# Loading the first weight chunks and inputs of both output stages from the stages ahead of them

## The reference, cut to what matters

```python
# first block
b = multiscale_pool(u_b, pool_w[layer], pool_scale[layer]) * jax.nn.silu(z_b)
g = jax.nn.sigmoid(gates.reshape(B, S, N_BRANCHES, D_MODEL) + merge_bias[layer])
y = g[:, :, 0] * (a @ w_branch_a[layer]) + g[:, :, 1] * (b @ w_branch_b[layer])
x = x + y @ w_out[layer]
# second block
merged = gate_a * (y_a @ w_proj_a[l]) + gate_b * (y_b @ w_proj_b[l])
y = merged @ w_out[l]
x = x + gate * _rms(y, g_post[l])
```

## Time and profile before

| | before |
|---|---|
| median of three runs | 3318.81 us (3316.91 to 3326.31) |
| profiled execution, its own time | 3323.57 us |
| its span | 3321.8 us |
| mean granted TensorE clock | 0.967 of full speed |
| PE busy | 3110.3 us, 94% |
| DVE, ACT, POOL busy | 1732.5, 1552.3, 956.3 us |
| out1 begins, out2 begins (SP's first DMA) | 1491.21, 2943.02 us |

### The profile page before, as it was taken

The page is one execution under the profiler, slowest core; times in us unless marked ns, Lnnn a source line. Parts: engine busy times, 40 slices in busy tenths (PEclk is TensorE's granted clock), DMA queues, the critical chain, the costliest instruction groups (busy, mean ns, idle before and its releaser), DMA issues. The chain is left out here.

```text
span 3321.8 us, 43017 instructions
## 1 busy us (share of the span) xinstructions
PE 3110.3 (94%) x15772; PEld 2529.6 (76%) x15772; DVE 1732.5 (52%) x3657; ACT 1552.3 (47%) x2448; POOL 956.3 (29%) x701
## 2 busy tenths in 40 slices
PE   8995999889995999997999799979999999989998
PEld 7994888768884677765778678868888888868787
DVE  6775799989996665536531166642211231133423
ACT  4544688756983677762111143324444354431111
POOL 3541012200222566642222133312322222212222
PEclk9996999999997999998999899989999999999999
DMA  5656333253334621106552345464344543355422
GB/s 177 206 182 231 96 96 100 80 189 110 100 102 155 198 78 51 39 20 192 155 146 93 131 150 161 140 212 142 114 131 137 197 125 118 119 152 157 133 102 89
DMA packets 431706, 440.63 MB, mean 133 GB/s; under 512 B 31008, under 2 KB 324256, under 8 KB 431392
## 3 DMA queue, kind: packets, MB, share of 16 engines
q1 hardware_dynamic: 431520, 438.18, 42.7%
HBM read 279.51 MB, written 158.60 MB: 132 GB/s over the span
## 5 line engine op out<-in xcount | busy, mean ns | idle before, releaser
L1342 PE MATMUL p_pr<-p_hT,p_w_hi 128*128 128x512 f32 x896 | 354.8, 396 | 16.1 <-POOL p_w_lo L1095 10.0
L1343 PE MATMUL p_pr<-p_hT,p_w_hi 128*128 128x512 f32 x896 | 352.3, 393 | 0.0
L1344 PE MATMUL p_pr<-p_hT,p_w_lo 128*128 128x512 f32 x896 | 352.0, 393 | 0.0
L1628 POOL TENSOR_TENSOR a_prob<-a_prob,a_inv 128x1024 f32<-128x1024 f32 (+12 forms) x104 | 250.7, 2419 | 211.2 <-DVE a_inv L1673 211.0
L1135 ACT ACTIVATE p_relu<-p_isc,p_level 128x2048 int8<-128x2048 f32 (+5 forms) x192 | 276.4, 1441 | 22.5 <-DVE p_level L1232 17.7
L791 PE MATMUL t_pj_ps<-t_w_hi,t_hT_slot 128*128 128x356 f32 (+2 forms) x768 | 272.2, 354 | 11.5 <-DVE t_w_lo L639 5.9
L1095 POOL TENSOR_TENSOR p_w_lo<-p_w_raw,p_w_hi 128x256 fp32r<-128x256 f32 x144 | 107.5, 777 | 603.7 <-DVE p_level L1232 399.6
L793 PE MATMUL t_pj_ps<-t_w_hi,t_hT_slot 128*128 128x356 f32 (+2 forms) x768 | 265.2, 345 | 0.0
L792 PE MATMUL t_pj_ps<-t_w_lo,t_hT_slot 128*128 128x356 f32 (+2 forms) x768 | 264.8, 345 | 0.0
L1648 DVE CUSTOM_DVE_ANT_0 a_prob<-a_s_ps,a_mask 128x512 f32<-128x512 f32 (+3 forms) x320 | 189.4, 607 | 141.2 <-PE a_s_ps L1782 136.5
L2260 PE MATMUL o_b_ps<-o_in_hi,o_w_hi 128*128 128x512 f32 x512 | 209.0, 408 | 39.5 <-DVE o_in_lo L2147 27.4
(11 more groups left out here) (291 smaller groups left out, 7120.4 us busy)
## 6 DMA issues: line engine op xcount, KB each, us to landing
s_hT<-t_hT_slot SPq DMA_DIRECT2D x32, 1024.0 KB, 5.9
s_gT<-p_o_sb SPq DMA_DIRECT2D x128, 256.0 KB, 4.9
o_gates<-s_gT SPq DMA_DIRECT2D x64, 512.0 KB, 5.1
p_w_raw<-in_w_in SPq DMA_DIRECT2D x56, 512.0 KB, 4.3
t2n_w_raw<-in_w_in SPq DMA_DIRECT2D x56, 512.0 KB, 4.2
s_qT<-t_qT_slot SPq DMA_DIRECT2D x32, 512.0 KB, 2.7
p_hT<-s_hT SPq DMA_DIRECT2D x32, 512.0 KB, 9.3
s_zuT<-p_o_sb SPq DMA_DIRECT2D x64, 256.0 KB, 4.8
```

Of the source, the lines that this page charges most:

```text
L1342: nc.tensor.matmul(pr[n % NPR][:], wh, hi, start=(k == 0), stop=False)
L1343: nc.tensor.matmul(pr[n % NPR][:], wh, lo, start=False, stop=False)
L1344: last = nc.tensor.matmul(pr[n % NPR][:], wl, hi, start=False, stop=(k == KD - 1))
L1628: nc.gpsimd.tensor_tensor(p, p, f, ALU.mult).then_inc(normed, 1)
```

## The change

1. The raw weights `w_raw` (32 KB a partition) and raw inputs `in_raw` (24 KB) of the output stages now lie at the start of the free memory, and are set aside in att1 and in second too, so that they cover tiles that die there: `w_ada`, `kT` and `qT` in att1, `hT0` and the split weights in second (for which `hT0` is now put ahead of them).
2. att1's SP, ahead of its last two stores, waits for all scores and then loads weights chunks 0 to 3 and a inputs 0 to 3 of out1: 8 + 4 DMAs of 256 KB. second's SP does the same for out2 ahead of its last three stores of gates, behind a wait for the last unit that reads `hT0` and for the last weight split.
3. The output stages don't load these any more. In out1 SP's order becomes: four u's (with the pooling weights behind the first), z 0 and 1, gates 0 and 1, z 2 and 3 (which wait for the first two mixes), chunks 4 to 7, four a inputs, and then at once the next group's u's and z 0, 1. For later groups the u's are issued in the turn of the last unit of the group before, one turn earlier than before.
4. In out2 the first four units now run as in out1, a halves first, and ACT and DVE split in the order that this needs.

```diff
+OPEN = 4
+RING = KD + KD // 2
+def merge_raw(c, tag):
+    with ExitStack() as shared:
+        sb, _, _ = c.alloc(shared, tag)
+        return sb("w_raw", [P, KD, D], F32), sb("in_raw", [P, RING, BANK], F32)
+def load_merge_weights(c, sp, n, second, landed):
+    for half, w in enumerate((c.w_proj_a_2, c.w_proj_b_2) if second else (c.w_branch_a, c.w_branch_b)):
+        sp.dma_start(c.merge_raw[0][:, half * KD // 2:(half + 1) * KD // 2, n * P:(n + 1) * P],
+                     w[0, :, n * P:(n + 1) * P].rearrange("(k p) n -> p k n", p=P)).then_inc(landed, 16)
+def load_merge_ahead(c, sp, second):
+    w_landed, a_landed = c.ahead[second]
+    for n in range(OPEN):
+        load_merge_weights(c, sp, n, second, w_landed[n])
+        sp.dma_start(c.merge_raw[1][:, n], c.aT[n][:, 0:BANK]).then_inc(a_landed[n], 16)
...
+                if turn == N_TURNS - 2:
+                    sp.wait_ge(scored, PIECES[N_TURNS])
+                    for s in (0, 1):
+                        sp.wait_ge(stored[s], 16 * GROUPS * NKV // 2)
+                    load_merge_ahead(c, sp, False)
                 sp.wait_ge(gated, turn + 1)
...
             if not second:
-                load_u(0, 0)
-                load_u(0, 1)
-            load_weights(0)
-            for x in range(KD):
-                load_src(x)
-            if not second:
-                sp.dma_start(w_pool.rearrange("c (g d) -> c g d", g=KB - 1), c.pool_w[0, 0:KB - 1].rearrange("g c d -> c g d")
-                             ).then_inc(wp_loaded, 16)
-                sp.dma_start(w_pool_last[:], c.pool_w[0, KB - 1]).then_inc(wp_loaded, 16)
-                load_weights(1)
-                load_u(0, 2)
-                load_u(0, 3)
+                for g in range(KB):
+                    load_u(0, g)
...
                 load_z(0, 0)
                 load_z(0, 1)
-            else:
-                load_weights(1)
+            for x in range(KB, KD):
+                load_src(x)
             load_gates(0)
-            load_weights(2)
             load_gates(1)
-            for n in range(3, KD):
-                load_weights(n)
             if not second:
                 load_z(0, 2)
                 load_z(0, 3)
+            for n in range(OPEN, KD):
+                load_weights(n)
             for x in range(KD, RING):
                 load_src(x)
+            if not second:
+                load_pool(1)
...
-                if not second and u < LAST and u % KD == 0:
-                    for g in range(KB):
-                        load_u(u // KD + 1, g)
-                    load_z(u // KD + 1, 0)
-                    load_z(u // KD + 1, 1)
+                if not second and u < LAST - KD and u % KD == KD - 1:
+                    load_pool(u // KD + 2)
...
-                if x == KB and not second:
+                if x == KB:
                     for n in range(1, OPEN):
                         high_weights(n)
...
                 low_merge(0)
-                for x in ON_DVE:
-                    low_input(x)
-                for n in range(1, KD):
+                low_input(0)
+                low_input(2)
+                for n in range(1, OPEN):
+                    low_merge(n)
+                low_input(4)
+                low_input(6)
+                for n in range(OPEN, KD):
                     low_merge(n)
...
-                if tg == 0 and not second:
-                    open_units(0, range(OPEN), 0)
+                if tg == 0:
+                    open_units(0, range(OPEN), None if second else 0)
...
+                if n == N_UNITS - 1:
+                    sp.wait_ge(unit_done, N_UNITS - LEAD)
+                    sp.wait_ge(w_lo_done, 2 * CHUNKS)
+                    for s in (0, 1):
+                        sp.wait_ge(a_stored[s], 16 * GROUPS * NKV // 2)
+                    load_merge_ahead(c, sp, True)
```

More of the change, by code:

```diff
@@ L208, in handed_on @@
     sb, _, _ = c.alloc(stack, name)
+    hT = [sb("hT0", [P, 2, KD, BANK], F32R)]
     w_raw = sb("w_raw", [P, 2, KD, P], F32)
@@ L211, in handed_on @@
     w_lo = sb("w_lo", [P, 3, KD, P], F32R)
-    hT = [sb(f"hT{g}", [P, 2, KD, BANK], F32R) for g in range(2)]
+    hT.append(sb("hT1", [P, 2, KD, BANK], F32R))
     return w_raw, w_hi, w_lo, hT
+OPEN = 4
[13 more added lines that the diff above has]
+        sp.dma_start(c.merge_raw[1][:, n], c.aT[n][:, 0:BANK]).then_inc(a_landed[n], 16)
 def pipeline(eng, stages, weights=None, later=None, ending=None):
@@ L1875, in phase_output @@
     tag = "r2" if second else "r1"
+    w_raw, in_raw = c.merge_raw
+    w_lo = sb("w_lo", [P, KD, D], F32R)
+    in_lo = sb("in_lo", [P, RING, BANK], F32R)
     yT = sb("yT", [P, T, KD, P], F32)
     w_hi = sb("w_hi", [P, KD, D], F32R)
-    with ExitStack() as shared:
-        w_raw = c.alloc(shared, tag)[0]("w_raw", [P, KD, D], F32)
-    w_lo = sb("w_lo", [P, KD, D], F32R)
     src = sb("src", [P, 2, BANK], F32)
@@ L1896, in phase_output @@
     x_out = gates[:].rearrange("p s b n -> p s (b n)")
-    w_loaded, w_hi_done, w_lo_done = [sem(f"w_loaded{n}") for n in range(KD)], sem("w_hi_done"), sem("w_lo_done")
-    raw_loaded = [sem(f"raw_loaded{x}") for x in range(RING)]
+    w_landed, a_landed = c.ahead[second]
+    w_loaded, w_hi_done, w_lo_done = w_landed + [sem(f"w_loaded{n}") for n in range(OPEN, KD)], sem("w_hi_done"), sem("w_lo_done")
+    raw_loaded = a_landed + [sem(f"raw_loaded{x}") for x in range(KB, RING)]
     src_loaded, g_loaded = [sem("s_even"), sem("s_odd")], [sem("g_even"), sem("g_odd")]
@@ L1966, in load_weights @@
             def load_weights(n):
-                for half, w in enumerate((wa, wb)):
-                    sp.dma_start(part(w_raw, n)[:, half * KB:(half + 1) * KB],
-                                 w[0, :, n * P:(n + 1) * P].rearrange("(k p) n -> p k n", p=P)).then_inc(w_loaded[n], 16)
+                load_merge_weights(c, sp, n, second, w_loaded[n])
             def load_gates(u):
@@ L1998, in load_z, with load_pool @@
                 sp.dma_start(z_pool[g % 2], c.zuT[8 + g][:, r * BANK:(r + 1) * BANK]).then_inc(z_loaded[g % 2], 16)
-            if not second:
-                load_u(0, 0)
-                load_u(0, 1)
-            load_weights(0)
-            for x in range(KD):
-                load_src(x)
-            if not second:
-                sp.dma_start(w_pool.rearrange("c (g d) -> c g d", g=KB - 1), c.pool_w[0, 0:KB - 1].rearrange("g c d -> c g d")
-                             ).then_inc(wp_loaded, 16)
-                sp.dma_start(w_pool_last[:], c.pool_w[0, KB - 1]).then_inc(wp_loaded, 16)
-                load_weights(1)
-                load_u(0, 2)
-                load_u(0, 3)
+            def load_pool(r):
+                for g in range(KB):
+                    load_u(r, g)
+                load_z(r, 0)
+                load_z(r, 1)
+            if not second:
+                for g in range(KB):
+                    load_u(0, g)
+                    if g == 0:
+                        sp.dma_start(w_pool.rearrange("c (g d) -> c g d", g=KB - 1), c.pool_w[0, 0:KB - 1].rearrange("g c d -> c g d")
+                                     ).then_inc(wp_loaded, 16)
+                        sp.dma_start(w_pool_last[:], c.pool_w[0, KB - 1]).then_inc(wp_loaded, 16)
                 load_z(0, 0)
                 load_z(0, 1)
-            else:
-                load_weights(1)
+            for x in range(KB, KD):
+                load_src(x)
             load_gates(0)
-            load_weights(2)
             load_gates(1)
-            for n in range(3, KD):
-                load_weights(n)
             if not second:
@@ L2102, in _ @@
                 if x == KD:
-                    for n in range(1 if second else OPEN, KD):
+                    for n in range(OPEN, KD):
                         high_weights(n)
@@ L2294, in _ @@
             for tg in range(GROUPS):
-                if tg == 0 and not second:
-                    open_units(0, range(OPEN), 0)
-                    pool_map(0, 2)
-                    pool_map(0, 3)
+                if tg == 0:
+                    open_units(0, range(OPEN), None if second else 0)
+                    if not second:
+                        pool_map(0, 2)
+                        pool_map(0, 3)
                     close_units(0, range(OPEN), None)
@@ L2381, in phase_second @@
     SCORES_AT, KEYS_AT, WEIGH_AT = 6, 9, 10
+    c.merge_raw = merge_raw(c, "r2")
     handed_on(c, stack, "p2n")
@@ L2786, in build_program @@
     c.x = c.x.rearrange("o s d -> (o s) d")
+    c.ahead = [([nc.alloc_semaphore(f"w_landed{second}{n}") for n in range(OPEN)],
+                [nc.alloc_semaphore(f"a_landed{second}{n}") for n in range(OPEN)]) for second in range(2)]
     with ExitStack() as keep:
```

8 lines of the change are left out of this document (2 added, 6 removed).

## The result

| | before | changed |
|---|---|---|
| median of six runs each, taken together | 3321.03 us (3316.91 to 3328.23) | 3305.16 us (3303.17 to 3308.65) |
| profiled execution, its own time | 3323.57 us | 3305.27 us |
| its span | 3321.8 us | 3303.5 us |
| mean granted TensorE clock | 0.967 | 0.969 |
| PE busy | 3110.3 us | 3107.1 us |

The changed kernel is faster by 15.9 us, a ratio of 0.995 with a 95% interval of 0.9939 to 0.9961. (out1's opening is from here on DVE's first instruction in it, 0.07 us behind SP's first DMA; out2's is SP's first DMA.)

A forecast was written before the change was run, and what follows sets the result against it. Out1's opening was taken as limited by late loads, splits and pooling, its body by PE. Gains of 16.3 us in out1 and 6.2 in out2 made 22.5, off 3318.8: 3296.3 us, own range 3292 to 3304, overall 3288 to 3308.

The forecast's parts named there:

- the wait for u: In out1's first group, DVE's 6.67 us wait for the next group's first u was to go.
- A: Rival: out1's stall only moves; chunk 7 lands 6 us later, gain 10 instead of 16; 3302.3 us, chance 0.14.
- the first product: DVE's first gate product in out1, forecast near 33 us after the opening.
- B: Rival: only the earlier starts of out1 and out2 are gained, 11 us; 3308 us, chance 0.11.
- the fifth product: DVE's fifth gate product in out1, forecast near 53 us after the opening.
- C: Rival: early loads hold att1's last store of `aT`, so att1 ends 33 us late; 3329 us, chance 0.03.
- D: Rival: early loads wait until their stage's end and land where they did; 0 to -6 us, 3316 us, chance 0.04.
- the collision: DVE and POOL splitting inputs together after each stage start: 0 extra taken, at most 3.0 us on DVE's chain in out1.
- The restart: PE's slow restart at out1's opening, kept as it was; staying at 2.4 GHz would give 2.7 us.

The follow-up runs named there:

- a: The changed kernel run again with no edit: 3304.99 us, 0.995 of before.
- i: The changed kernel run a third time, unaltered: 3302.7 us, 0.9941 of before.
- h: The kernel before the change, run once more: 3316.3 us (one run).
- c: The changed kernel with the change undone in att1 and out1, so kept for out2 only: 3315.77 us, 0.998 of before.
- b: The changed kernel with the change undone in second and out2, so kept for out1 only: 3308.78 us, 0.9962 of before.
- e: The changed kernel with all four first-group a inputs split on DVE, none on POOL, in both output stages: 3300.23 us, 0.9938 of before.
- f: The changed kernel with POOL's splits of out1's second-group a inputs held until the stage's sixth mix is done: 3300.54 us, 0.9939 of before.

## Why the prediction was right, and where its sum was off

**The mechanism held.** The early loads are issued where they should be, ahead of the stores and at no cost to them; ACT starts with the stage; the wait for u is gone; out1 and out2 add up. A is not there: ACT waits 0.85 us for chunk 7, until 1522.48, and the first product is 30.9 us after the opening, ahead of the 32.7 forecast, mostly because the late chunks landed 4.8 us after their issue and not 6.1. B is out by the fifth product, 15.1 us earlier against the opening, C by the 3.40 us between att1's last product and out1's opening, D by the loads.

**By stages.** In the two profiles the gain is 18.3 us of the 22.5 that the sum took off the profiled execution: out1 14.8 for 16.3, out2 6.0 for 6.2, and the stages ahead of out1 lost 2.5 for 0. The mean of three profiles on each side (changed, a and i; as before, out1 also in h and c, out2 also in h and b) makes it 14.0 in out1 and 5.6 in out2, about 3 us short of the sum.

**The term that was wrong is the collision, taken as 0.** The prediction had "the other end is two POOL splits waited for in full, 3.0 us", and gave as its reason that out1 before had the same meeting. It read that meeting too narrowly. In the kernel before, POOL's two first splits held up one DVE split (1.25 us for 0.68) and the pooling step right behind it (1.76 for 0.69), 1.6 us in all. There ACT delivered inputs one by one as they landed; with everything in memory all four arrive at once, the two DVE splits take 3.46 us (four took 2.49 in e, so two should take 1.25), and the pooling step takes 0.68. So DVE loses 2.2 us, little more than before, but now all of it ahead of the first matmul, which is 1.0 us late in both stages. In out1 this is made up by the last input split of the first unit, 25.6 us after the opening for 25.5 forecast.

The second meeting is the costlier one, and the prediction did not look for it: the next group's a inputs are split by POOL while DVE sums the first unit and pools. Those three instructions take 5.24 us for 2.07 (3 by 0.69), 3.2 more. Of these, 1.1 are the sum, which was as slow before; the prediction took it at the speed that it has beside an idle POOL ("1524.0 + 1.9 = 1525.9"). The other 2.1 are the pooling steps, taken at 1.63 from a stretch in which POOL was idle; the change itself brings them into POOL's splits by taking away the wait for the u. That the miss stayed small is partly luck: the first product came 1.8 us early, mostly by the faster landings, so the fifth is only 1.4 late, 54.0 where 52.6 was forecast. e and f remove one meeting each. The Trainium skill (SBUF — State Buffer, section SBUF: two separate sides) says that GpSimd and a VectorE operation with two operands in SBUF exclude each other for whole instructions. The runs bear it out here nearly in full: from the start of POOL's four splits to the end of DVE's third instruction 7.0 us pass, and four splits (2.53 us for two, with DVE on other work) and three instructions of 0.69 make 7.1. The prediction was wrong to trust the partial collision of the earlier trace rows over it.

**The restart.** I kept the slow restart of PE as it was and counted 14 matmuls at 1.2 GHz. In the changed kernel's out1, 8 matmuls stood 0.41 us or more ahead of the next after the idle 7.53, and the first 24 took 7.6 us where the prediction had 8.3 (14 by 0.43, 10 by 0.23), so 0.7 us came back. It isn't the same each time: in a the count was 9 in out1 and 13 in out2, in i 11 and 12.

**The median.** The prediction subtracted from 3318.8, the median of three runs; the later medians of before were 3321.0 to 3322.1. The changed kernel is 15.9, 17.0 and 19.4 us below the one taken with it, 17.4 on average, so about 5 us of the sum are missing, about 3 of them in the two output stages, and 2.2 of the 8.9 us between forecast and time come from that starting point.

**What stays open: the stages ahead of out1.** out1 opened at 1491.28, 1487.87 and 1490.75 in the three profiles without early loads for it, and from 1489.10 to 1493.79 in the ten with them, 1491.6 on average for 1490.0. With such a spread that difference of 1.6 us can't be told from none. In one turn of the changed kernel's profile the loss can be seen, though. PE before:

```profile
1169.80 1.13 PE L1839 MATMUL a_side<-a_area,keep_ident 128*128 128x256 f32 x4 [0.70 <-DVE a_area L1706]
```

and in the changed kernel:

```profile
1162.40 1.03 PE L1871 MATMUL a_side<-a_area,keep_ident 128*128 128x256 f32 x4
1163.36 1.95 PE L1839 MATMUL a_o_ps<-a_pt,a_v 128*64 128x256 f32 x16
...
1171.14 2.07 PE L1871 MATMUL a_side<-a_area,keep_ident 128*128 128x256 f32 x4 [2.92 <-DVE a_area L1738]
```

The load behind it is one of 512 KB. Its row among the DMA issues from 1158 to 1172 before:

```profile
a_area<-in_b_ada SPq DMA_DIRECT2D x1, 512.0 KB, 5.7
```

and in the changed kernel:

```profile
a_area<-in_b_ada SPq DMA_DIRECT2D x1, 512.0 KB, 7.9
```

It landed 2.2 us later, some 290 us ahead of anything that the change issues. The wait of 2.92 us is followed by four matmuls in 2.07 us for 1.13. From the first load of keys to the last product att1 takes 443.1, 444.6 and 444.8 us without early loads, 448.9, 445.9 and 445.7 in the changed kernel, and 442.2 to 445.9 in the seven others that have its att1 unchanged (mean 443.6). That speaks against a cost of the moved tiles and for chance; it was not tested alone, and about 2 us of the sum stay without a cause.

## What to carry to other kernels

When a change makes operands ready sooner, list which engines then work in the same memory at the same time, and read the length of every instruction in that stretch of the trace before, also where it was hidden by a wait: a DVE instruction with two SBUF operands and a POOL instruction were no parallel work here, so a split shared between them was slower than DVE alone (2.49 us for four against 3.46 for two beside POOL's two). A gain at a stage's opening is kept only by what is late next, so follow it to the last unit of the opening, and look at one more thing than the wait that goes: what then runs in its place, and beside what. Compare stages by opening-to-opening lengths of several profiles; two of one kernel were 3 us apart.

## What was not expected of the hardware

- TensorE's slow restart was not the same each time. Over the thirteen profiles 6 to 14 matmuls stood 0.41 us or more ahead of the next (0.43 is 512 columns at 1.2 GHz) in the twenty openings with 6.5 to 8.7 us of idle time ahead, and 12 or 13 in the six with 12.3 to 12.9 us, in three of which a wait for a weight split ends the count. In the changed kernel the granted clock was 0.52 from 1497.87 to 1501.87 and 1.00 from 1502 on.
- Both engines paid for a meeting, DVE most of it: its sum of 128x512 went from 0.69 to 1.79 us, while POOL's four splits took 6.47 us beside DVE's three instructions and 5.47 in f, where they came later. DVE's gate product, which has one operand in PSUM, took 1.22 us inside POOL's splits and 1.23 outside.
- A load of 512 KB landed 2.2 us later in one execution than in another, in a stretch where both programs do the same work.
